# Memory's keys and values in a block on one core: plain fp32 products of raw weight tiles, and a new order of loads and sums in the front

## What is computed

```python
# first block, front
mod = silu(c) @ w_ada + b_ada            # 2048 x 12288 weights, one row of c
h = rms_norm(x, g_norm1) * (1 + sc1) + sh1
proj = h @ w_in                          # 2048 x 3904
# second block
mem_n = rms_norm(mem, mem_norm_g)        # 256 x 2048
k = mem_n @ xa_wk                        # 2048 x 1024
v = mem_n @ xa_wv                        # 2048 x 1024
```

## Time and profile before

| | |
|---|---|
| median of three runs | 2275.51 us |
| the profiled execution | 2278.13 us |
| its span | 2276.4 us |
| TensorE busy (matmul) | 2129.4 us, 94% |
| VectorE busy | 1548.4 us, 68% |
| ScalarE busy | 993.5 us, 44% |
| mean transfer rate | 215 GB/s |
| mean granted clock of TensorE | 0.978 |

### The profile page before, as it was taken

One profiled execution on the slowest core, in us unless ns is written; L12 is line 12 of the kernel. 1 busy time (PEld: TensorE's weight loads), 2 busy tenths in 40 slices (PEclk: granted clock), 3 DMA queues, 4 the chain that ended last, 5 costly groups with the idle time before them and its releaser, 6 DMA issues.

```text
span 2276.4 us, 26435 instructions
## 1 busy us (share of the span) xinstructions
PE 2129.4 (94%) x9726; PEld 1733.8 (76%) x9726; DVE 1548.4 (68%) x1699; ACT 993.5 (44%) x1270; POOL 161.2 (7%) x227
## 2 busy tenths in 40 slices
PE   3789997768989999999999999998999999999998
PEld 2578886547768888888888888887787878888887
DVE  5889987676877755555545556489778788865554
ACT  5235545542353344434444454533344444444443
POOL 2000002100000000000000006130202000000000
PEclk9999998888999999999999999999999999999999
DMA  9997983428878866557666556665455555657654
GB/s 332 402 358 256 382 292 111 139 81 308 314 245 282 279 211 193 187 194 212 192 187 189 194 207 208 180 179 172 141 155 158 177 177 170 197 186 239 186 190 151
DMA packets 223265, 490.21 MB, mean 215 GB/s; under 512 B 15322, under 2 KB 17728, under 8 KB 221872
## 3 DMA queue, kind: packets, MB, share of 16 engines
q1 hardware_dynamic: 218080, 467.20, 62.4%
q0 software_dynamic: 4112, 17.16, 2.2%
q10 hardware_dynamic: 960, 4.35, 0.5%
HBM read 482.35 MB, written 6.29 MB: 215 GB/s over the span
## 4 chain that ended last, share of the span: by engine, by line
PE 70%; DVE 7%; ACT 3%; DMA 2%; issue 1%; POOL 0%; DVEq 0%; ACTq 0%; SPq 0%; POOLq 0%
PE psum L548 64%; DVE w_lo L1807 2%; ACT w_hi L1188 1%; DMA raw<-in_w_gate 1%; DVE acc L1827 1%; DMA raw<-in_w_out 1%; PE psum L910 1%; PE psum L950 1%; PE psum L718 1%; PE psum L505 1%; PE psum L1159 0%; PE psum L743 0%; PE psum L962 0%; DVE st L2420 0%; PE psum L813 0%
## 5 line engine op out<-in xcount | busy, mean ns | idle before, releaser
L1807 DVE TENSOR_TENSOR w_lo<-raw,w_hi 128x1024 fp32r<-128x1024 f32 x698 | 856.7, 1234 | 594.7 <-ACT w_hi L1188 585.8
L1188 ACT ACTIVATE w_hi<-raw 128x1024 fp32r<-128x1024 f32 (+1 forms) x698 | 734.4, 1056 | 1102.3 <-PE psum L548 890.2
L548 PE MATMUL psum<-w_hi,x_hi 128*128 128x512 f32 (+1 forms) x2048 | 816.8, 399 | 41.5 <-DVE w_lo L1807 38.7
L548 PE MATMUL psum<-w_lo,x_hi 128*128 128x512 f32 (+1 forms) x2048 | 800.9, 391 | 0.0
L548 PE MATMUL psum<-w_hi,x_lo 128*128 128x512 f32 (+1 forms) x2048 | 800.5, 391 | 0.0
L548 PEld LDWEIGHTS psum<-w_hi,x_hi 128*128 128x128 f32 x2048 | 388.3, 190 | 139.1 <-DVE w_lo L1807 40.7
L548 PEld LDWEIGHTS psum<-w_lo,x_hi 128*128 128x128 f32 x2048 | 387.9, 189 | 82.0
L548 PEld LDWEIGHTS psum<-w_hi,x_lo 128*128 128x128 f32 x2048 | 388.8, 190 | 77.7 <-issue 1.0
L548 PE MATMUL psum<-w_hi,f_hi 128*128 128x512 f32 x352 | 137.7, 391 | 0.0
L548 PE MATMUL psum<-w_lo,f_hi 128*128 128x512 f32 x352 | 137.1, 389 | 0.0
L548 PE MATMUL psum<-w_hi,f_lo 128*128 128x512 f32 x352 | 137.0, 389 | 0.0
(11 more groups left out here) (376 smaller groups left out, 1729.0 us busy)
## 6 DMA issues: line engine op xcount, KB each, us to landing
raw<-in_w_in SPq DMA_DIRECT2D x264, 512.0 KB, 4.1
ring<-in_w_ada SPq DMA_DIRECT2D x144, 512.0 KB, 6.1
raw<-in_w_gate SPq DMA_DIRECT2D x88, 512.0 KB, 3.7
raw<-in_w_up SPq DMA_DIRECT2D x88, 512.0 KB, 3.7
raw<-in_w_down SPq DMA_DIRECT2D x88, 512.0 KB, 3.6
raw<-in_w_out SPq DMA_DIRECT2D x64, 512.0 KB, 3.7
raw<-in_w_ada SPq DMA_DIRECT2D x48, 512.0 KB, 4.5
raw<-in_w_branch SPq DMA_DIRECT2D x48, 512.0 KB, 4.1
```

The source lines that it names most:

```text
L548: last = pe.matmul(pair(b)[:, a, 0:width], x[:, k, cut], w[:, s, kk, 0:width], start=(u == 0 and kk == 0 and n == 0), stop=(u == units - 1 ...
L1188: act.activation(w_hi[:, s, :, 0:width], raw[:, r, :, 0:width], ACT.Copy).then_inc(hi_ready, 1)
L1807: dve.tensor_tensor(w_lo[:, s, :, 0:width], raw[:, r, :, 0:width], w_hi[:, s, :, 0:width].bitcast(F32), ALU.subtract).then_inc(raw_used, 1)
```

## The change

- Memory's tokens are turned raw, without norm and without a split: ScalarE writes the turned chunk times the gain to a new buffer `mem_T`. The units multiply `mem_T` by `raw` itself in plain fp32, 4 products per unit instead of 12, and count on a new semaphore `mem_used`, which frees the slot of `raw`. The norm of the tokens is applied to the keys and values when they are copied out (`copy_mem`).
- The order of loads is `MEM_ORDER`: eight b, four g, twelve times "bgbgb", twenty b, four g, four b. The number of tiles is as before.
- The first sum stands after memory's unit 10, the second after 21, the third after 28, the fourth behind the 64th fold, ahead of x's chunks; memory's last four units stand behind x's first four chunks.
- On VectorE the small operations are placed among the folds: the first part of the rows after fold 20, the line of the bias after fold 24, the second part of the rows after fold 44.
- The DMA of memory's tokens is issued on ScalarE's queue right behind the row c, ahead of the other rows. x's tokens are issued after memory's chunks. The junk of the squares goes to `x_hi`, `k_tok` is a half of `m_tok`.

```diff
+MEM_UNITS = 4 * (D // 2 // P)
+MEM_ORDER = "bbbbbbbb" + "gggg" + "bgbgb" * 12 + "b" * 20 + "gggg" + "bbbb"
+MEM_SUMS = {10: 0, 21: 1, 28: 2}
 # SP
+                    s = pl.slot("raw", SLOTS)
+                    sp.wait_ge(mem_used, pl.at("raw", 1))
+                    name, k, c, width = next(src)
+                    sp.dma_start(raw[:, s, :, :], views[name][:, k:k + 2, c:c + width]).then_inc(landed[s], 16)
...
-            load("bbbbgggg", ahead)
-            load("b" * KD)
-            for m in range(3):
-                load(B2, ahead)
-            load(G8 + N0, ahead)
+            load_mem(MEM_ORDER, ahead)
+            load("gggg" + N0, ahead)
 # TensorE
+                    pe.wait_ge(landed[r], pl.landed())
+                    for a in range(TT):
+                        for kk in range(2):
+                            last = pe.matmul(pair(b)[:, a, :], mem_T[:, 2 * u + kk, a * P:(a + 1) * P], raw[:, r, kk, :],
+                                             start=(u == 0 and kk == 0), stop=(u == 7 and kk == 1))
+                    last.then_inc(mem_used, 1)
...
+            pe.wait_ge(mem_in, 16)
+            operand_ready()
+            before_mem = pl.n["chunk"]
+            for u in range(4):
+                turn_chunk(m_tok, before_mem, u)
+            for u in range(8):
+                pe.wait_ge(chunks_taken, 2 + before_mem + u + 1)
+                multiply_mem(1)
+                if u + 4 < 8:
+                    turn_chunk(m_tok, before_mem, u + 4)
             pe.wait_ge(small_in, 16 * SMALL_DMAS)
             pe.wait_ge(heads_spread, 1)
             pe.matmul(psum[:, 7, :], rb_wide[:, :], onehot[:, :], start=True, stop=True).then_inc(line_summed, 1)
...
+            multiply_mem(20)
+            multiply(MEM_ORDER.replace("g", ""))
             sum_ada()
...
+            pe.wait_ge(line_set, 1)
             pe.wait_ge(x_scaled, 2)
-            turn_and_multiply(x_tok, ["gb"] * 6 + ["g"] * 2, between=lambda: multiply(G8[4:]))
+            turn_and_multiply(x_tok, ["gb"] * 6 + ["g"] * 2, between=lambda: multiply_mem(4))
 # ScalarE
+            for u in range(8):
+                act.wait_ge(chunks_turned, pl.at("chunk", 1))
+                for j in range(2):
+                    last = act.activation(mem_T[:, 2 * u + j, :], psum[:, 4 + u % 4, j * SEQ:(j + 1) * SEQ], ACT.Identity,
+                                          scale=col("mem_g", 2 * u + j))
...
+                    last = act.activation(dst[:, a, :], pair(p)[:, a, :], ACT.Copy, scale=stats[:, 0, a:a + 1])
 # VectorE
-            work("bbbb")
+            work("b" * 6)
             plain([(b_cols[:, :], 0, 96), (cols[:, KD:], P + KD, NROWS - KD)])
...
+            work("b" * 16)
+            take_ada(1)
             dve.wait_ge(sines_set, 1)
...
-            work("ggg")
+            work("b" * 16)
+            take_ada(2)
+            work("b" * 4)
+            pl.step("block", 4)
+            pl.step("raw", MEM_UNITS)
+            take_ada(3)
```

More of the change, by code:

```diff
@@ L388, in walk, with load_mem @@
                     k += 2
+            def load_mem(seg, src):
+                for kind in seg:
+                    if kind == "b":
+                        load("b")
+                        continue
+                    s = pl.slot("raw", SLOTS)
+                    sp.wait_ge(mem_used, pl.at("raw", 1))
+                    name, k, c, width = next(src)
+                    sp.dma_start(raw[:, s, :, :], views[name][:, k:k + 2, c:c + width]).then_inc(landed[s], 16)
+                    pl.step("raw")
             def load(seg, src=None):
@@ L579, in sum_ada, with turn_chunk, multiply_mem @@
                 pl.step("ada")
+            def turn_chunk(x, before, u, ready=None):
+                if u >= 4:
+                    pe.wait_ge(chunks_taken, 2 + before + u - 3)
+                if ready:
+                    ready(u)
+                for j in range(2):
+                    for a in range(TT):
+                        last = pe.transpose(psum[:, 4 + u % 4, (2 * j + a) * P:(2 * j + a + 1) * P],
+                                            x[:, a, (2 * u + j) * P:(2 * u + j + 1) * P], ident[:, :])
+                last.then_inc(chunks_turned, 1)
+                pl.step("chunk")
+            def multiply_mem(units):
+                for _ in range(units):
+                    n = pl.n["raw"]
+                    u, b, r = n % 8, pl.slot("block", 2), pl.slot("raw", SLOTS)
+                    if u == 0:
+                        pe.wait_ge(pair_taken[b], pl.n["block"] // 2 + 1)
+                    pe.wait_ge(landed[r], pl.landed())
+                    for a in range(TT):
+                        for kk in range(2):
+                            last = pe.matmul(pair(b)[:, a, :], mem_T[:, 2 * u + kk, a * P:(a + 1) * P], raw[:, r, kk, :],
+                                             start=(u == 0 and kk == 0), stop=(u == 7 and kk == 1))
+                    last.then_inc(mem_used, 1)
+                    pl.step("raw")
+                    if u == 7:
+                        pl.step("block")
+                    if n + 1 in MEM_SUMS:
+                        sum_ada()
             def turn_and_multiply(x, kinds, ready=None, between=None):
@@ L585, in turn_and_multiply @@
                 pe.wait_ge(ada_taken, pl.at("ada", 1))
[L587 to L597, removed]
                 for u in range(4):
-                    turn_chunk(u)
+                    turn_chunk(x, before, u, ready)
                 if between:
@@ L608, in turn_and_multiply @@
                     if u + 4 < 8:
-                        turn_chunk(u + 4)
+                        turn_chunk(x, before, u + 4, ready)
             pe.wait_ge(c_in, 16 * 2)
@@ L1233, in copy_out, with copy_mem @@
                 pl.step("block")
+            def copy_mem(dst, block):
+                p = pl.slot("block", 2)
+                act.wait_ge(mem_used, SLOTS + 8 * (block + 1))
+                for a in range(TT):
+                    last = act.activation(dst[:, a, :], pair(p)[:, a, :], ACT.Copy, scale=stats[:, 0, a:a + 1])
+                last.then_inc(pair_taken[p], 1)
+                pl.step("block")
             def taken_count(p):
@@ L1895, in row @@
                 return sm[:, k, :]
[L1897 to L1918 removed]
+            work("b" * 6)
+            pl.step("norm", 2)
+            work("b" * 4)
             dve.wait_ge(dt_ready, 1)
```

108 lines of the change are left out of this document (42 added, 66 removed).

## The result

The changed kernel took 2282.34 us, the median of nine runs (2276.03 to 2285.16), beside 2273.06 us for the kernel before (nine runs, 2269.71 to 2277.83). The ratio of the two is given as 1.0025, with a 95% interval from 1.0015 to 1.0035, which is some 6 us slower (3.4 to 8.0). The two medians themselves are 9.3 us apart, or 0.41%, more than that interval; which of the two is nearer isn't settled by these runs. The kernel is certainly not faster, and by the ratio it lies within the 0.3% that I had called no difference, though the interval's upper end lies just over it. The profiled execution has a span of 2280.5 us against 2276.4. These spans are only 4.1 us apart, since the profiled execution of the kernel before (2278.13 us) was slower than each of its nine timed runs, while that of the changed kernel is its median. What follows accounts for the 4.1 us.

The account below looks back on a forecast made before the run. Loads, then TensorE, bound the front; TensorE alone behind 181 us. Early units, waits, SSM rows, folds and tail put x's start at 182.9 against 182.65 us, +0.2: 2276 us on the median's footing, own range 2270 to 2282, whole 2267 to 2288.

Parts of the forecast that it names:

- Start of the units: Memory's first unit on TensorE starts at about 24 us, after the sixth fold, the column copy and four slow turns.
- End of unit 23: TensorE's memory units, 3.45 us each: T = 115 us without waits, 120 with one wait of 3.5 and a slow clock.
- rival (b): Slower, chance 0.18: transfers reach only 336 GB/s up to unit 23, T = 128; 2284 us, or 2288 with a slow tail.
- The 44th fold: VectorE's fold after unit 23 frees its load: data in 5.2 us, fold 1.4.
- The SSM rows: VectorE's rows, hidden before, now stand between the 44th and 45th fold and cost 6.9 us.
- The 20 folds: Folds 45 to 64 before the fourth sum: 1.39 us each, 27.8 in all, VectorE setting the pace.
- The tail: From the 64th fold to x's first unit: sum, take, turns, memory's last four units and slow clock, 21.6 us.
- Behind x's start nothing changes: From x's first product of w_in to the end, the program keeps the same length as before.
- Rival (a): Faster, chance 0.32: TensorE never waits and the tail is warm; T = 115, x at 175.3 us, 2268 us.
- Rival (c): Chance 0.03: memory's units never get the full clock on plain fp32; a unit takes 6.9 us, T 83 later.
- Rival (d): Chance 0.05: units miss the 24 us start through late rows or waiting chunks; 10 us late gives 2284 or so.
- the page's rule: HBM limit of about 358 GB/s per core; if it held from 31 us on, T would be 122.

Follow-up runs that it names:

- e4: Changed kernel with the bias line's copy and 2.1 MB write after the 44th fold instead of the 24th; 2277.06 us, ratio 1.0006 to the kernel before.
- e1: Changed kernel with VectorE's second part of the SSM rows moved behind x's first low part; 2273.55 us, ratio 0.9995 to the kernel before.
- e3: Changed kernel with memory's last four units loaded among folds 45 to 52 and multiplied before the fourth sum; 2271.05 us, ratio 0.9983 to the kernel before.
- e8: Changed kernel with the DMA of memory's tokens put back behind the small row DMAs; 2280.61 us, ratio 1.0025 to the kernel before.
- e2: Changed kernel with five ring slots instead of four, buffers placed anew; 2272.89 us, ratio 0.9991 to the kernel before.
- e6: Changed kernel with all memory units before the fourth sum and the SSM rows after fold 28, four slots; 2268.37 us, ratio 0.9975 to the kernel before.
- the combined one: Changed kernel with five slots, early units, SSM rows after fold 28, line after fold 44, first w_in tile split early; 2261.15 us, ratio 0.9948.

## Why the prediction was right in size, and where its steps failed

The time forecast was 2276 us and the median is 2282.3; by the ratio the change costs 6 us, where I had 0.2. The time lies inside the whole range (2267 to 2288), but just above the forecast's own (2270 to 2282), so a term was off. Of the 6.3 us, 4.0 lie between the profiled executions (2282.34 against the 2278.3 of my sum), and the steps below account for them. The other 2.3 are what I took off to get from the profiled execution to the median: the kernel before had been profiled in a slow execution and the changed one wasn't. By the steps, in their order:

- **Start of the units, 24.1 us forecast, 24.95 measured.** The chain was right: the sixth fold (19.75 to 21.03), the copy of the columns, four turns at the slow clock (21.51 to 24.95, 3.4 us).
- **End of unit 23, T = 120 forecast, 118.8 measured** (SP's queue issues the last of the 28 tiles at 118.77). The units are 3.43 us apart (SP's queue issues a weight tile for each, at 111.91, 115.34 and 118.77 us), as priced from two lone products. TensorE waited 2.8 us for weight tiles, forecast 3.5, but in three pieces and without falling to the slow clock. That it was the line's write is shown by e4, in which these waits are gone. From 31 to 119 us 390 GB/s were moved, above the 368 under which rival (b) would have decided.
- **The 44th fold, T + 6.6 at its end forecast, 126.90 us measured, T + 8.1.** Its tile was issued at 119.2 us and landed 6.4 us later, where I had 5.2 for it from the 3.6 us of the earlier trace rows. So this is the same error as in the folds below. In e1, e3 and e8 the fold starts 6.8 us behind the last of the 28 tiles too. That the T was 1.2 us earlier and nearly cancels it is luck.
- **The SSM rows, 6.9 us forecast, 6.8 measured**, and e1 shows that this is what they cost.
- **The 20 folds, 27.8 us forecast, 32.0 measured. This is the main step that failed.** I wrote that "four ring slots with a way round of 3.6 + 1.4 us allow one per 1.25, so VectorE sets the pace". The 3.6 us were a tile of `in_w_down` from a part of the kernel where the transfers are half idle. A ring tile in this stretch takes 5.5 us, and four slots then allow one fold per 1.7 us. Part 6 of the page of the kernel before, from which I had the 3.6, also has the row of the ring tile itself:

```profile
ring<-in_w_ada SPq DMA_DIRECT2D x144, 512.0 KB, 6.1
```

  With 6.1 us in the place of 3.6 the same formula gives (6.1 + 1.39)/4 = 1.87 us per fold: 30.0 for the 16 that aren't loaded ahead, and with 5.5 for the first four 35.5. The middle between that and 27.8 would have put x at 186.8 us, but to take the middle is a choice made after the result. e2 shows the cause: with one slot more the stretch is 27.6 us.
- **The tail, 21.6 us forecast, 21.15 measured**, with the sum at the slow clock (3.58), the turns 3.4 and the units 13.7 us.
- **Behind x's start nothing changes**: 1928.4 us against 1929.0 behind the `staged` turn.

The ledger of x's start, measured less forecast: +0.2 us up to the 45th fold (T -1.2, the 44th fold +1.5, the rows -0.1), +4.2 for the folds, -0.45 for the tail, together the 3.9 us between 182.9 and 186.8. The landing time of a ring tile, priced at 3.6 us where it is 5.5 to 6.4, thus cost 5.7 us of forecast, and two smaller errors took part of it back. That the change brings nothing was right for the reason given: the early start of the units is real, but the front ends with VectorE's folds; the rows were put into their way and the last units behind them.

Rival (a) fell on T, as TensorE did wait for 2.8 us, and on the tail, which wasn't warm: 23 us of idle time stood before the sum. Rival (c) fell plainly: a unit stayed at 3.43 us on plain fp32 products alone, at a granted clock of 1.00. Rival (b) has the nearest sum, 2284, by a mechanism that didn't happen: T wasn't late, and the 390 GB/s up to it are above its 336. Rival (d) fell with the start at 24.95 us. Windows of the changed kernel from the first units to T and over the fold run, then of e2_ring5 over its fold run (columns as above):

```profile
31.00:119.00 88.00, 85.23 (x229) 39.29 (x228) 42.38 (x48) 19.24 (x27) 4.26 (x6) 1.00 1.00 390
...
134.00:166.00 32.00, 3.83 (x18) 3.75 (x18) 24.89 (x21) 0.00 (x0) 0.00 (x0) 0.54 0.87 297
```

```profile
131.00:159.00 28.00, 3.69 (x17) 3.61 (x17) 25.40 (x22) 0.00 (x0) 0.00 (x0) 0.57 0.90 328
```

**On the page's rule.** In the changed kernel too, 406 GB/s were moved from 60 to 119 us, with a DMA share of 1.03. The Trainium skill, page DMA: Bandwidth & Descriptors, section Specifications, has about 358 GB/s for one core's share of HBM. As a limit for a core that runs alone, as here, it is exceeded again, and the measurement decides; how two cores share isn't shown by any run here. The same page, section Anatomy of one DMA, gives 2.0 us and the bytes at 436 GB/s for one transfer, a fit of another kind of queue than this one. An estimate by it is 3.2 us for 512 KB. That is near the 3.5 us of `in_w_down` and far from the 5.5 us of a ring tile with three others under way, so for the pace of a ring it is a bound from below and no price.

**What stays open.** The medians put the loss at 9.3 us and the ratio at 5.7, while the traces account for 4.2. e6's median lies 5 us above its profiled execution, and its trace can't say where another run of it loses that time; with it stays open why the gains of e1 and e3 don't add up in the times. No run has the buffers of e2 with four slots.

## What to carry to other kernels

Price a ring by slots and by the landing time of its own tile in its own stretch, (landing + use)/slots against the use: here 1.7 against 1.39 us, and a fifth slot was worth 4.4 us over 20 tiles. When work is moved early on a full engine, ask whose last event opens the next stage; work that stands before that event on the same engine (the rows, 6.8 us) costs its full length, and so does nearly all that stands between it and the stage (four units of 13.7 us, whose removal shortened the tail by 11.6), while behind x's first chunks (the rows in e1) it was free. And a transfer that was free in one order (the line's write in e4, in a hole of the transfers) is to be tried again in the combined one, where the hole is gone and it cost 4.9 us.

## What the runs showed of the hardware

The landing time of a 512 KB tile isn't a constant. It is 3.5 us for `in_w_down`, 5.5 (3.4 to 9.8) for ring tiles at 297 GB/s with four slots, and 5.3 at 328 GB/s with five: one more slot gave more throughput at no longer landing time. A write of 2.1 MB in a stretch where the transfers run at a share of 1.03 took 14.6 us to land and stopped TensorE for 2.8 us in the changed kernel. It took 8.5 us and stopped nothing where the ring's full slots had left the transfers at a share of 0.40 (e4). And the clock: TensorE came back from waits of 1.53 us at full speed (3.70 us for the eight products, 3.60 without a wait), while after 23.00 us of idle time the sum took 3.58 us, twice the 1.84 of the one inside the units.
